# The recurrent block's norm scale applied to projection results instead of to the rows

## The chip, the core and the metric

One core of one Trainium2 chip runs the whole program once. The time is the device time of that core in microseconds (us), the median of several executions; one execution is profiled. The engines are TensorE (PE, with its weight loads as PEld), VectorE (DVE), ScalarE (ACT), GpSimd (POOL) and SyncE (SP, which only issues DMAs here). Each runs its own instructions in order, and they meet at semaphores. Matmul results land in eight PSUM banks.

## What is computed

Two blocks follow each other on x, 256 tokens by 1024 features, float32. Block 1 has two attention layers, each of which ends in `x = x + gate * rms_norm(y, g_post[l])`. Block 2 begins with a recurrent mixer, its feed-forward part, then a second layer with eight experts and a final norm. The place of the change is the seam between layer 1 of block 1 and the recurrent mixer:

```python
def rms_norm_2(x, g):
    y = x * rsqrt(mean(x * x, axis=-1) + EPS)
    return y * g

h = x                                             # what block 1 returned
hn = rms_norm_2(h, norm_mix[0])
proj = hn @ ev_w_in                               # 1024 -> 2568
xr, yr, q, k, v, f_logit = jnp.split(proj, EVEN_SPLITS, axis=-1)   # five of 512, one of 8
xc = causal_depthwise_conv(xr, conv_w, conv_b)    # 4 taps along the tokens
h_lru = rglru(xc, ...)                            # two gates per channel, then a scan over tokens
y_a = h_lru * gelu(yr)
log_f = log_sigmoid(f_logit + f_b)
y_b = fox_attention(q, k, v, log_f)               # 8 heads, cumsum(log_f) added to the scores
h = h + concatenate([y_a, y_b]) @ w_out
```

The norm's factor 1/sqrt(mean + EPS) is one number for each token, so it can be put on the rows before the product or on its result.

## The kernel before

Activations lie transposed, features on partitions: `x`, `h` and their like are eight tiles (k = 0 to 7) of 128 features by 256 tokens. Products are made from two parts of each operand: ACT copies a tile to the reduced type fp32r (the upper part, `hi`), DVE subtracts to get the rest (`lo`), and PE adds three products (`product`, L801 to L805: hi by hi, lo by hi, hi by lo). Weights stream from memory through `ring`, six slots of 1 MB filled by SP. A slot of 256 output columns gives two pieces of 128 columns. `piece_upper(n)` is ACT's part of piece n (L1766) and `piece_lower(n)` DVE's (L2840). Four pairs of part tiles are used in turn (PIECES = 4): ACT may form piece n only when PE is done with piece n-4, and PE starts a projection when its `lo` part is there.

The order on each engine is written out by hand, one section per engine. The PSUM banks are claimed in turn from two groups of four, "gemm" and "attn" (`claim`, L721): PE waits until the last user of the bank has been read by the engine named with the claim.

At the seam the order is this. PE ends layer 1's eight output tiles ("out"), forms the mean of squares of the result ("post") and spreads its inverse root over the partitions (`spread`, L774). DVE multiplies `yo` by it and adds it to `x`, in four pairs of tiles (L2834, L2838). Then comes the norm of the mixer: DVE forms h = x * weight (`weighted`, L2857) for all tiles, ACT the squares (L1763), PE their mean per token (`token_squares`, L763), ACT the root, DVE the reciprocal, PE spreads it. Then h is scaled in place in four pairs (`normed`, L2867), ACT forms their upper parts (`pair_uppers`, L1802) and DVE their lower ones (L2871). In between PE runs idle products on constants (`keep_busy`, L788). After that PE projects: flog (8 outputs spread over 128 rows, plain float32, L748), then xr, yr, qf in four chunks each, the two gates of the recurrence ("lru", 8 small products), kf in four chunks, and vf in two. Each chunk of xr, yr, qf, kf is 24 matmuls into one bank.

Results leave PSUM on ACT (`copy_out`, L1821, and `rows_out`, L2065 and L2066, which puts two heads of 64 rows apart), each followed on ACT by the `piece_upper` that PE's next chunks need. Before the first copy ACT issues nine DMAs for later (`fetch`, L1721: mask, picks, gate weights). DVE meanwhile convolves xr (`convolve`, L2899 and L2901), works on flog and its running sum (L2915 to L2917), and forms the lower parts between these. POOL forms gelu's argument from yr (L3440 to L3444).

## Time and profile before

| | us |
|---|---|
| median of 3 runs | 1960.36 |
| lowest, highest | 1958.73, 1962.9 |
| the profiled execution | 1962.08 |
| its span, first to last instruction | 1958.8 |
| mean granted TensorE clock | 0.988 |

The profile is of one execution. "Busy" is the time in which an engine executes; the time before an instruction in which its engine stood idle is given with what released it. All times below count from the first instruction. The seam lies at 638 to 656 us, the mixer's projections at 656 to 723 us.

### The profile page before, as it was taken

Reading aid. Unit: us, or ns where it says so; the run is one execution under the profiler, and the core shown is the slowest. Engines: PE = TensorE matmul, PEld = TensorE weight load, DVE = VectorE, ACT = ScalarE, POOL = GpSimd, SP = SyncE. Lnnn points to the kernel's source line nnn. Section 1 sums busy time; section 2 is a strip of 40 time slices with the busy share of each in tenths; the row PEclk is TensorE's granted clock in tenths of the full one; section 3 lists DMA queues with packets and bytes.
Section 4 is the critical chain, followed back from the end, with each engine's and each line's share of the span. In section 5 each row is a group of like instructions: output and inputs, shape, how many; then the busy total and the mean of one; then the engine's idle time right before and its main releaser. Section 6 shows DMA issues by size and latency. Waiting matters only on the chain.

```text
span 1958.8 us, 30650 instructions
## 1 busy us (share of the span) xinstructions
PE 1918.3 (98%) x12361; PEld 1570.0 (80%) x12361; DVE 1185.5 (61%) x1698; ACT 969.5 (49%) x1429; POOL 29.8 (2%) x29
## 2 busy tenths in 40 slices
PE   6999999999999999999999999999999999999998
PEld 4999899999899989999999736883588887368833
DVE  4767886565785776666663217951498884059611
ACT  3647753466863575443463206740476673057501
POOL 1000000000000120000000000000000000000000
PEclk7999999999999999999999999999999999999999
DMA  9985556465544542555455899999999999999997
GB/s 291 270 267 184 163 174 160 98 188 189 158 140 140 177 142 88 194 194 158 158 187 203 336 395 407 416 365 412 409 413 409 404 374 347 414 408 411 409 410 303
DMA packets 292565, 536.83 MB, mean 274 GB/s; under 512 B 67076, under 2 KB 198600, under 8 KB 278096
## 3 DMA queue, kind: packets, MB, share of 16 engines
q1 hardware_dynamic: 287968, 530.82, 75.4%
q10 hardware_dynamic: 3920, 3.69, 0.6%
q8 instruction: 98, 1.61, 0.3%
q0 software_dynamic: 544, 0.43, 0.1%
q14 instruction: 35, 0.29, 0.0%
HBM read 533.83 MB, written 1.07 MB: 273 GB/s over the span
## 4 chain that ended last, share of the span: by engine, by line
PE 62%; DMA 2%; DVE 1%; ACT 1%; issue 0%; SPq 0%; DVEq 0%
PE bank L803 14%; PE bank L805 14%; PE bank L804 13%; PE bank L1603 9%; PE bank L1630 4%; DMA pool<-in_od_exp_w 2%; PE bank L1411 1%; PE bank L1458 1%; PE bank L1487 1%; PE bank L1519 1%; PE bank L763 1%; PE bank L748 1%; PE bank L1616 0%; PE bank L788 0%; PE bank L779 0%
## 5 line engine op out<-in xcount | busy, mean ns | idle before, releaser
L3123 DVE TENSOR_TENSOR expert_lo<-pool,w_hi 128x2048 fp32r<-128x2048 f32 x168 | 376.9, 2287 | 46.6 <-ACT w_hi L2268 46.5
L2268 ACT ACTIVATE w_hi<-pool 128x2048 fp32r<-128x2048 f32 x168 | 313.2, 1912 | 29.4 <-DMA pool<-in_od_exp_w 25.3
L803 PE MATMUL bank<-h_upper,upper 128*128 128x256 f32 x1056 | 310.0, 294 | 2.1 <-DVE ring_lo L2537 2.0
L804 PE MATMUL bank<-h_lo,upper 128*128 128x256 f32 x1056 | 300.5, 285 | 0.0
L805 PE MATMUL bank<-h_upper,ring_lo 128*128 128x256 f32 x1056 | 300.4, 284 | 0.0
L2537 DVE TENSOR_TENSOR ring_lo<-ring,upper 128x1024 fp32r<-128x1024 f32 x148 | 179.7, 1222 | 102.9 <-ACT upper L1785 102.6
L803 PEld LDWEIGHTS bank<-h_upper,upper 128*128 128x128 f32 x1056 | 204.1, 193 | 9.6 <-issue 8.5
L804 PEld LDWEIGHTS bank<-h_lo,upper 128*128 128x128 f32 x1056 | 204.3, 193 | 1.0 <-issue 0.4
L805 PEld LDWEIGHTS bank<-h_upper,ring_lo 128*128 128x128 f32 x1056 | 204.1, 193 | 0.0
L1603 PE MATMUL bank<-pool,xe_light 128*64 128x512 f32 (+1 forms) x976 | 187.4, 539 | 2.8 <-issue 2.0
L2847 DVE TENSOR_TENSOR piece_lo<-ring,piece_hi 128x1024 fp32r<-128x1024 f32 x118 | 144.7, 1237 | 73.9 <-ACT piece_hi L1774 73.6
L803 PE MATMUL bank<-w_hi,xe_hi 128*128 128x512 f32 x448 | 178.0, 397 | 2.9 <-DVE expert_lo L3123 2.9
L1785 ACT ACTIVATE upper<-ring 128x1024 fp32r<-128x1024 f32 x148 | 155.1, 1054 | 41.8 <-DMA ring<-in_w_in 24.7
L805 PE MATMUL bank<-w_hi,xe_lo 128*128 128x512 f32 x448 | 174.9, 390 | 0.0
L804 PE MATMUL bank<-expert_lo,xe_hi 128*128 128x512 f32 x448 | 174.3, 389 | 0.0
L1603 PEld LDWEIGHTS bank<-pool,xe_light 128*64 128x64 f32 x976 | 69.1, 137 | 108.4 <-issue 99.3
L1774 ACT ACTIVATE piece_hi<-ring 128x1024 fp32r<-128x1024 f32 x118 | 123.1, 1053 | 51.4 <-PE bank L805 51.2
L803 PEld LDWEIGHTS bank<-w_hi,xe_hi 128*128 128x128 f32 x448 | 84.3, 188 | 24.3 <-DVE expert_lo L3123 4.6
L1630 PE MATMUL bank<-pool,hT_light 128*64 128x512 f32 x448 | 99.9, 594 | 0.0
L803 PE MATMUL bank<-row_hi,piece_hi 128*128 128x256 f32 x352 | 99.9, 284 | 0.0
L804 PE MATMUL bank<-row_lo,piece_hi 128*128 128x256 f32 x352 | 99.6, 283 | 0.0
L805 PE MATMUL bank<-row_hi,piece_lo 128*128 128x256 f32 x352 | 99.6, 283 | 0.0
(482 smaller groups left out, 3605.0 us busy)
## 6 DMA issues: line engine op xcount, KB each, us to landing
pool<-in_od_exp_w SPq DMA_DIRECT2D x330, 1024.0 KB, 13.9
ring<-in_w_in SPq DMA_DIRECT2D x48, 1024.0 KB, 5.7
ring<-in_ev_ffn_w SPq DMA_DIRECT2D x33, 1024.0 KB, 5.3
ring<-in_w_ada SPq DMA_DIRECT2D x24, 1024.0 KB, 7.7
ring<-in_od_w_in SPq DMA_DIRECT2D x12, 1024.0 KB, 5.4
ring<-in_ev_w_in SPq DMA_DIRECT2D x10, 1024.0 KB, 5.4
ring<-in_w_in SPq DMA_DIRECT2D x32, 256.0 KB, 4.5
ring<-in_w_out SPq DMA_DIRECT2D x8, 1024.0 KB, 4.9
```

Source lines behind the costliest of these rows:

```text
L748: m = nc.tensor.matmul(b[base:base + rows, 0:cols], left(k), right(k), start=(k == 0), stop=(k == K - 1))
L803: nc.tensor.matmul(b, left[0], right[0], start=first, stop=False, skip_group_check=True)
L804: nc.tensor.matmul(b, left[0], right[1], start=False, stop=False, skip_group_check=True)
L805: return nc.tensor.matmul(b, left[1], right[0], start=False, stop=last, skip_group_check=True)
L1603: m = nc.tensor.matmul(b[ROOM * j:ROOM * j + ROOM, 0:cols_], xe_light[:, c], t[:, k, cols_ * j:cols_ * j + cols_], start=c == 0, stop=c == ...
L1630: m = nc.tensor.matmul(bank[Y[0]][ROOM * n:ROOM * n + ROOM], t[:, e, ROOM * j:ROOM * j + ROOM], w[:, k, 512 * n:512 * n + 512], start=blk ...
L1774: nc.scalar.activation(piece_tiles(n, *src.shape[1:])[0], src, ACT.Copy)\
L1785: nc.scalar.activation(upper_tile(n), upper_source(n)[0], ACT.Copy)\
L2268: nc.scalar.activation(w_hi[q % HIS], ring_slot(q), ACT.Copy)\
L2537: V.tensor_tensor(dst, src, upper_tile(n).bitcast(F32), ALU.subtract)\
L2847: V.tensor_tensor(lo, src, hi.bitcast(F32), ALU.subtract).then_inc(piece_ready, tick(piece_ready, n))
L3123: V.tensor_tensor(low_slot(q), ring_slot(q), w_hi[q % HIS].bitcast(F32), ALU.subtract)\
```

## The change

The rows of the mixer are no longer scaled. h = x * weight goes into the products as it is, and every result is multiplied by the token's factor when it leaves PSUM. This moves work:

- DVE takes the exits of flog, xr, yr, qf and kf from ACT (`rows_out`, `head_rows_out`, a multiplication of the bank by `rstd[:, 0]`). ACT keeps those of vf, with the factor as its scale, in two halves per tile. ACT's copy of the factor to SBUF is new (`row_root`).
- The four xr chunks are run together, input tile by input tile, each in its own bank, as soon as the parts of a pair of tiles are there (`project_weighted`). The mean of squares is formed between them. flog and the spreading of the factor come after.
- DVE forms h and the lower parts behind each pair of sums of x (`after_sum`). ACT does square and upper part pair by pair.
- The parts of the first four pieces are formed by ACT while the output tiles 3 to 6 of layer 1 run, and by DVE ahead of and behind the reciprocal of "post".
- Piece 4 is formed before, pieces 5 to 7 behind ACT's nine DMAs.
- `yo` gets a place of its own, over the finished gates za and zb, and three banks are claimed from "attn" in place of "gemm".

```diff
@@ -225,7 +225,8 @@
-    z = {b: place(4, S) for b in "abc"}
+    yo = place(8, S)
+    z = {"a": yo[:, 0:4], "b": yo[:, 4:8], "c": place(4, S)}
...
-    yo = qkc
...
-        def spread(key, first, n, freed_by, *step):
+        def spread(key, first, n, freed_by, *step, group="gemm"):
-            b = claim("gemm", ("r", *key, first), freed_by, *step)
+            b = claim(group, ("r", *key, first), freed_by, *step)
...
-        token_squares(("mix", 0))
-        keep_busy(4)
-        spread(("mix", 0), 0, NT, h_ready, "mix", 0, KD - 1)
-        keep_busy(5)
+        def project_weighted(key, *targets):
+            banks = [claim("gemm", (name, c), scaled_rows, name, c) for name, c, _ in targets]
+            for k in range(KD):
+                pe.wait_ge(left_ready, when(left_ready, *key, k))
+                for b, (name, c, tile) in zip(banks, targets):
+                    w = take_piece((tile,), c % 2, KD, P)
+                    m = product(b[:, 0:S], [t[:, k] for t in w], (left_hi[:, k], left_lo[:, k]), k == 0, k == KD - 1)
+                    if k == KD - 1:
+                        m.then_inc(psum_ready, wrote(name, c))
+                        release_piece((tile,), c % 2)
+                mean_square_part(key, k, "attn")
+
+        project_weighted(("mix", 0), *(("xr", c, "xr" + "1" * (c // 2)) for c in range(4)))
         pe.wait_ge(flog_spread, when(flog_spread, "all"))
-        chunk(("flog",), "gemm", clog_ready, ("flog",), KD, lambda k: flogw[:, k], lambda k: h[:, k],
-              fresh=("mix", 0))
+        b = claim("attn", ("flog",), clog_ready, "flog_rows")
+        for k in range(KD):
+            if k == KD // 2:
+                spread(("mix", 0), 0, NT, rstd_row, "mix", 0, group="attn")
+            m = nc.tensor.matmul(b[:, 0:S], flogw[:, k], h[:, k], start=(k == 0), stop=(k == KD - 1))
+        m.then_inc(psum_ready, wrote("flog"))
 
             for c in range(4):
-                project_piece((name + "1" * (c // 2),), c % 2, (name, c), proj_ready,
-                              fresh=("mix", 0) if (name, c) == ("xr", 0) else None)
-
-        project_rows("xr")
+                project_piece((name + "1" * (c // 2),), c % 2, (name, c), scaled_rows)
+
         project_rows("yr")
         project_rows("qf")
...
@@ -2035,17 +2047,20 @@
                     .then_inc(yo_ready, tick(yo_ready, "out", l, c))
                 if c < KD - 1:
                     form_behind(("out", l, c // 2), c % 2)
+                if l == L - 1 and 2 < c < KD - 1:
+                    piece_upper(c - 3)
             token_root("post", l)
-
-        pair_squares(("mix", 0), x, lambda k: (x_ready, when(x_ready, "l", L - 1, k)))
-        for n in range(2):
-            piece_upper(n)
+        for c in range(0, KD, 2):
+            act.wait_ge(x_ready, when(x_ready, "l", L - 1, c + 1))
+            nc.scalar.activation(sq[:, c:c + 2], x[:, c:c + 2], ACT.Square).then_inc(sq_ready, two(sq_ready, "mix", 0, c))
+            act.wait_ge(weighted_step, when(weighted_step, "l", L - 1, c + 1))
+            nc.scalar.activation(left_hi[:, c:c + 2], h[:, c:c + 2], ACT.Copy)\
+                .then_inc(left_hi_ready, two(left_hi_ready, "mix", 0, c))
         token_root("mix", 0)
-        pair_uppers(("mix", 0))
-        for n in range(2, PIECES):
-            piece_upper(n)
+        piece_upper(PIECES)
+        row_root("mix", 0, slot=0)
 
         act.wait_ge(psum_ready, when(psum_ready, "ms", "mix", 0))
         fetch(loaded_block2, mask, C["causal"][:, 0:P])
...
-        def rows_out(name, c, dst):
-            b = psum(act, name, c)
-            nc.scalar.activation(dst[0:HEAD, 0, c], b[0:HEAD, 0:S], ACT.Copy)
-            nc.scalar.activation(dst[HEAD:P, 1, c], b[HEAD:P, 0:S], ACT.Copy)\
-                .then_inc(proj_ready, tick(proj_ready, name, c))
...
-        for c in range(4):
-            copy_out(("xr", c), conv[:, c, 3:3 + S])
+        for c in range(1, 4):
             piece_upper(c + PIECES)
         act.wait_ge(clog_ready, when(clog_ready, "abs"))
         nc.scalar.activation(tmp[:, 0], tmp[:, 0], ACT.Exp, scale=-1.0).then_inc(lru_act, tick(lru_act, "fexp"))
         for c in range(4):
-            copy_out(("yr", c), yr[:, c])
             piece_upper(4 + c + PIECES)
         act.wait_ge(clog_ready, when(clog_ready, "one"))
         nc.scalar.activation(tmp[:, 0], tmp[:, 0], ACT.Ln).then_inc(lru_act, tick(lru_act, "fln"))
         for c in range(4):
-            rows_out("qf", c, qf)
             piece_upper(8 + c + PIECES)
...
-        rows_out("kf", 0, kf)
         piece_upper(12 + PIECES)
         act.wait_ge(lru_dve, when(lru_dve, "loga"))
         nc.scalar.activation(ag, rg, ACT.Exp).then_inc(lru_act, tick(lru_act, "a"))
-        rows_out("kf", 1, kf)
...
-            nc.scalar.activation(vf[:, :, 256 * j:256 * j + 256], b.rearrange("p (t n) -> p t n", t=NT), ACT.Copy)\
-                .then_inc(proj_ready, tick(proj_ready, "vf", j))
+            for t in range(NT):
+                m = nc.scalar.activation(vf[:, t, 256 * j:256 * j + 256], b[:, 256 * t:256 * t + 256], ACT.Copy,
+                                         scale=rtok[:, t:t + 1])
+            m.then_inc(proj_ready, tick(proj_ready, "vf", j))
...
+        def after_sum(c):
+            if c >= 0:
+                for k in (c, c + 1):
+                    weighted(vec("norm_mix_2", k), k, "l", L - 1)
+            if c > 0:
+                pair_lower(("mix", 0), c - 2)
+            if c == KD - 2:
+                pair_lower(("mix", 0), c)
+
+        def pair_lower(key, c):
+            pair = slice(c, c + 2)
+            dve.wait_ge(left_hi_ready, when(left_hi_ready, *key, c + 1))
+            V.tensor_tensor(left_lo[:, pair], h[:, pair], left_hi[:, pair].bitcast(F32), ALU.subtract)\
+                .then_inc(left_ready, two(left_ready, *key, c))
@@ -2826,7 +2865,13 @@
             if l == 0:
                 lower(*both("cq", l + 1), (("ckv", l + 1), 0))
                 shift_gain(1)
+            if l == L - 1:
+                for n in range(PIECES - 1):
+                    piece_lower(n)
             inverse_tokens("post", l)
+            if l == L - 1:
+                dve.wait_ge(psum_ready, when(psum_ready, "out", l, KD - 1))
+                piece_lower(PIECES - 1)
             r = spread_root("post", l)[:, 0:S]
             dve.wait_ge(yo_ready, when(yo_ready, "out", l, KD - 1))
...
-                .then_inc(weighted_step, tick(weighted_step, *ready, c))
+                if l == L - 1:
+                    after_sum(c - 2)
...
-        for c in range(KD):
-            weighted(vec("norm_mix_2", c), c, "l", L - 1)
-        piece_lower(0)
-        normed(("mix", 0), parts=True, behind=lambda: piece_lower(1))
-        for n in range(2, PIECES):
-            piece_lower(n)
+        inverse_tokens("mix", 0)
+        piece_lower(PIECES)
         link(V.memset(conv[:, :, 0:3], 0.0))
-
+        dve.wait_ge(rstd_row, when(rstd_row, "mix", 0))
+
+        def rows_out(name, c, *dsts):
+            b = psum(dve, name, c)
+            for rows, dst in dsts:
+                m = V.tensor_tensor(dst, b[rows, 0:S], rstd[rows, 0], ALU.mult)
+            m.then_inc(scaled_rows, tick(scaled_rows, name, c))
+
+        def head_rows_out(name, c, dst):
+            rows_out(name, c, *((slice(HEAD * e, HEAD * e + HEAD), dst[HEAD * e:HEAD * e + HEAD, e, c]) for e in range(2)))
+
+        every = slice(0, P)
+        for c in range(4):
+            rows_out("xr", c, (every, conv[:, c, 3:3 + S]))
+        piece_lower(1 + PIECES)
         b = psum(dve, "flog")
-        V.tensor_scalar(clog, b[:, 0:S], fb, None, ALU.add).then_inc(clog_ready, tick(clog_ready, "flog"))
+        V.tensor_tensor(clog, b[:, 0:S], rstd[:, 0], ALU.mult).then_inc(clog_ready, tick(clog_ready, "flog_rows"))
+        dve.wait_ge(clog_ready, when(clog_ready, "flog_rows"))
+        V.tensor_scalar(clog, clog, fb, None, ALU.add).then_inc(clog_ready, tick(clog_ready, "flog"))
         dve.wait_ge(clog_ready, when(clog_ready, "flog"))
...
         for c in range(4):
-            piece_lower(c + PIECES)
+            if c > 1:
+                piece_lower(c + PIECES)
             convolve(c)
         dve.wait_ge(lru_act, when(lru_act, "fexp"))
         V.tensor_scalar(tmp[:, 0], tmp[:, 0], 1.0, None, ALU.add).then_inc(clog_ready, tick(clog_ready, "one"))
         for n in range(4, 8):
+            rows_out("yr", n - 4, (every, yr[:, n - 4]))
             piece_lower(n + PIECES)
         dve.wait_ge(lru_act, when(lru_act, "fln"))
...
         for n in range(8, 12):
+            head_rows_out("qf", n - 8, qf)
             piece_lower(n + PIECES)
...
+        head_rows_out("kf", 0, kf)
         piece_lower(12 + PIECES)
...
         for n in range(13, 16):
+            head_rows_out("kf", n - 12, kf)
             piece_lower(n + PIECES)
...
-        pool_engine.wait_ge(proj_ready, when(proj_ready, "yr", 3))
+        pool_engine.wait_ge(scaled_rows, when(scaled_rows, "yr", 3))
         pool_engine.wait_ge(lru_dve, when(lru_dve, "conv", 3))
```

The functions `piece_lower`, `left_lower` and `weighted` are moved up in DVE's section, unchanged. Waits on `proj_ready` for the results that DVE now reads become waits on the new semaphore `scaled_rows`.

PE, from the spreading of "post" in layer 1 to xr. `ident,mean1024` are idle products, `mean1024,sq` the means of squares, `ident,small` spreads a factor, `h,pool` is flog. Before:

```order
L779 MATMUL bank0<-ident,small 128x128 x2
L788 MATMUL bank4<-ident,mean1024 128x128 x12
L763 MATMUL bank1<-mean1024,sq 128x1 x16
L788 MATMUL bank4<-ident,mean1024 128x128 x4
L779 MATMUL bank2<-ident,small 128x128 x2
L788 MATMUL bank4<-ident,mean1024 128x128 x5
L748 MATMUL bank3<-h,pool 128x256 x8
L803 MATMUL bank0<-left_hi,piece_hi 128x256
```

After, from the end of the last xr chunk to the first yr product:

```order
L806 MATMUL bank0<-left_hi,piece_lo 128x256
L764 MATMUL bank4<-mean1024,sq 128x1 x2
L1181 MATMUL bank5<-h,pool 128x256 x4
L780 MATMUL bank6<-ident,small 128x128 x2
L1181 MATMUL bank5<-h,pool 128x256 x4
L804 MATMUL bank1<-left_hi,piece_hi 128x256
```

The xr products stood behind flog and now stand ahead of it; their banks are 1, 2, 3 and 0, and bank 0 is the one in which the factor of "post" was spread. (A float32 product of the order is two in the trace.)

ACT, from the last root of layer 1 to the first exits. `small<-bank` is a root, `sq<-x` the squares, `left_hi` and `piece_hi` the upper parts of rows and of weights. Before:

```order
L1763 ACTIVATE sq<-x 128x512 x4
L1774 ACTIVATE piece_hi<-ring 128x1024 x2
L1812 ACTIVATE small<-bank1,small 128x2
L1802 ACTIVATE left_hi<-h 128x512 x4
L1774 ACTIVATE piece_hi<-ring 128x1024 x2
L1721 DMA pool<-const_causal 128x128
L1721 DMA pool<-const_pick 32x1024 x4
L1721 DMA pool<-in_ev_ga_w_2 64x4x64 x2
L1721 DMA pool<-in_ev_gx_w_2 64x4x64 x2
L1821 ACTIVATE pool<-bank0 128x256
L1774 ACTIVATE piece_hi<-ring 128x1024
```

The same place after (line numbers of the changed file):

```order
L2059 ACTIVATE left_hi<-h 128x512
L1824 ACTIVATE small<-bank4,small 128x2
L1786 ACTIVATE piece_hi<-ring 128x1024
L1809 ACTIVATE rstd<-bank6 128x256
L1733 DMA pool<-const_causal 128x128
L1733 DMA pool<-const_pick 32x1024 x4
L1733 DMA pool<-in_ev_ga_w_2 64x4x64 x2
L1733 DMA pool<-in_ev_gx_w_2 64x4x64 x2
L1786 ACTIVATE piece_hi<-ring 128x1024 x3
```

The nine DMAs now stand behind an instruction that needs the spread factor, and the parts of pieces 5 to 7 behind them.

DVE, from the last lower part of the rows to the second convolution. Before:

```order
L2847 TENSOR_TENSOR piece_lo<-ring,piece_hi 128x1024 x2
L2889 MEMSET pool 128x4x3
L2892 TENSOR_SCALAR pool<-bank,small 128x256
L2894 SCALAR_TENSOR_TENSOR tmp<-pool 128x256
L2847 TENSOR_TENSOR piece_lo<-ring,piece_hi 128x1024
L2899 TENSOR_SCALAR pool<-pool,vecs 128x256
L2901 SCALAR_TENSOR_TENSOR pool<-pool,vecs 128x256 x3
L2847 TENSOR_TENSOR piece_lo<-ring,piece_hi 128x1024
```

After:

```order
L2912 MEMSET pool 128x4x3
L2918 TENSOR_TENSOR pool<-bank,rstd 128x256 x4
L2540 TENSOR_TENSOR piece_lo<-ring,piece_hi 128x1024
L2929 TENSOR_TENSOR pool<-bank,rstd 128x256
L2931 TENSOR_SCALAR pool<-pool,small 128x256
L2933 SCALAR_TENSOR_TENSOR tmp<-pool 128x256
L2938 TENSOR_SCALAR pool<-pool,vecs 128x256
L2940 SCALAR_TENSOR_TENSOR pool<-pool,vecs 128x256 x3
L2938 TENSOR_SCALAR pool<-pool,vecs 128x256
L2940 SCALAR_TENSOR_TENSOR pool<-pool,vecs 128x256 x3
L2540 TENSOR_TENSOR piece_lo<-ring,piece_hi 128x1024
```

Ahead of the first convolution there are now four exits of xr and the lower part of piece 5; the lower parts of pieces 6 and 7 stand behind the second and the third convolution.

## Rows read from the trace of the kernel before

**Rows 1.** The page, busy time, share of the span and instructions, by engine.

```profile
PE 1918.3 (98%) x12361; PEld 1570.0 (80%) x12361; DVE 1185.5 (61%) x1698; ACT 969.5 (49%) x1429; POOL 29.8 (2%) x29
```

**Rows 2.** Stretches: length, busy (instructions) of PE, PEld, DVE, ACT, POOL; PEclk; DMA.

```profile
644.20:656.10 11.90, 11.46 (x71) 10.64 (x71) 11.20 (x23) 6.66 (x11) 0.95 (x1) 0.86 0.43 137
656.10:690.80 34.70, 34.70 (x290) 34.67 (x289) 28.87 (x37) 20.79 (x31) 9.85 (x5) 1.00 0.57 177
690.80:696.40 5.60, 3.60 (x19) 2.85 (x17) 3.38 (x6) 5.31 (x11) 5.52 (x2) 1.00 0.74 241
```

**Rows 3.** Timeline of PE: start, duration, line, count, [idle before <- releaser].

```profile
640.88 0.61 PE L779 MATMUL bank<-ident,small 128*128 128x128 f32 x4
641.33 2.84 PE L788 MATMUL bank<-ident,mean 128*128 128x128 f32 x24
...
652.82 3.62 PE L748 MATMUL bank<-h,pool 128*128 128x256 f32 x16
656.09 0.47 PE L803 MATMUL bank<-left_hi,piece_hi 128*128 128x256 f32 x1
```

**Rows 4.** Timeline of DVE at the seam, same columns.

```profile
641.53 1.28 DVE L2834 TENSOR_TENSOR pool<-pool,bank 128x512 f32<-128x512 f32 x2 [0.98 <-PE bank L779]
...
644.54 0.68 DVE L2834 TENSOR_TENSOR pool<-pool,bank 128x512 f32<-128x512 f32 x1
645.13 1.29 DVE L2838 TENSOR_TENSOR x<-x,pool 128x512 f32<-128x512 f32 x2
646.34 2.19 DVE L2857 TENSOR_SCALAR h<-x,vecs 128x256 f32<-128x256 f32 x8
```

**Rows 5.** Timeline of PE in layer 1's output tiles: a mean of squares among products.

```profile
624.80 0.28 PE L805 MATMUL bank<-h_upper,ring_lo 128*128 128x256 f32 x1
624.92 0.50 PE L763 MATMUL bank<-mean,sq 128*128 128x1 f32 x4
625.29 0.36 PE L803 MATMUL bank<-h_upper,upper 128*128 128x256 f32 x1
```

**Rows 6.** Timeline of PE, then stretches: a wait and the granted clock behind it.

```profile
123.01 0.36 PE L803 MATMUL bank<-h_upper,upper 128*128 128x256 f32 x1 [2.01 <-DVE ring_lo L2537]
...
124.14 0.42 PE L804 MATMUL bank<-h_lo,upper 128*128 128x256 f32 x1
124.35 0.41 PE L805 MATMUL bank<-h_upper,ring_lo 128*128 128x256 f32 x1
...
124.00:127.00 3.00, 3.00 (x16) 3.00 (x16) 2.96 (x5) 2.15 (x3) 0.00 (x0) 0.50 1.10 349
```

**Rows 7.** Timeline of ACT and its DMA issues (ACTq) before the first exit.

```profile
655.28 0.37 ACTq L1721 DMA_DIRECT2D pool<-const_causal  x1
...
659.70 1.41 ACTq L1721 DMA_DIRECT2D pool<-in_ev_gx_w  x2
661.16 0.38 ACT L1821 ACTIVATE pool<-bank 128x256 f32<-128x256 f32 x1 [3.43 <-issue]
```

**Rows 8.** Timeline of DVE during xr, yr and qf.

```profile
663.66 0.41 DVE L2899 TENSOR_SCALAR pool<-pool,vecs 128x256 f32<-128x256 f32 x1
664.11 1.53 DVE L2901 SCALAR_TENSOR_TENSOR pool<-pool,vecs 128x256 f32<-128x256 f32 x3
665.55 1.22 DVE L2847 TENSOR_TENSOR piece_lo<-ring,piece_hi 128x1024 fp32r<-128x1024 f32 x1
...
682.87 1.26 DVE L2915 SCALAR_TENSOR_TENSOR tmp<-pool,tmp 128x256 f32<-128x256 f32 x1
...
686.68 3.17 DVE L2847 TENSOR_TENSOR piece_lo<-ring,piece_hi 128x1024 fp32r<-128x1024 f32 x2
```

**Rows 9.** Timeline of PE around the gates and before vf.

```profile
694.71 1.99 PE L748 MATMUL bank<-pool 128*128 128x256 f32 x8 [2.00 <-ACT pool L2071]
696.36 0.47 PE L803 MATMUL bank<-left_hi,piece_hi 128*128 128x256 f32 x1
...
709.04 0.35 PE L803 MATMUL bank<-piece_hi,left_hi 128*128 128x256 f32 x1 [0.83 <-DVE piece_lo L2847]
```

38 lines of the change are left out of this document (19 added, 19 removed).

## The prediction

> **What bounds the kernel now.** I read the page's busy shares first: PE is busy 98% of the span, every other engine 61% or less [rows 1]. So time can be won or lost only where PE waits, runs filler, or runs slowly. Then I read the stretches around the seam. From 644.2 to 656.1 us PE is called busy for 11.46 of 11.9 us, yet none of it but the spreading and flog is work that a result needs: the rest is means of one column and idle products, at a granted clock of 0.86. DVE, busy 11.20 of 11.9 us, sets the pace [rows 2]. From 656.1 to 690.8 PE runs xr, yr and qf without a wait, and **DVE is already busy for 28.87 of these 34.7 us**, ACT for 20.79 [rows 2]. That is the number on which the forecast turns, since the change takes work off ACT and puts it on DVE. After that PE waits 2.00 us for ACT's first gate [rows 9]. Behind vf the order does not change much, and what the seam gains or loses is passed on: the weights of the experts are fetched when PE's progress lets them.
>
> **Part 1, the start of xr.** Now the first xr product starts at 656.09 [rows 3]. After the change it needs the parts of tiles 0 and 1 and four free banks, one of them the bank from which DVE reads the factor of "post" until its fourth yo product. DVE's chain now begins at 641.53; a pair product or sum costs 0.60 from start to start (645.13 minus 644.54), eight weightings 2.1, so 0.26 each [rows 4]. The lower part of piece 3 is put ahead of the chain where DVE stands idle for 0.98 us; it takes 1.22, so the chain starts 0.1 later, at 641.64. The fourth yo product, at 644.54 now, gets in front of it two weightings (0.52 and some 0.13 for a semaphore on DVE's own result), twice, and one lower part of a pair (0.60): 644.54 + 0.1 + 0.65 + 1.25 = 646.55, done at 647.25. The parts of tiles 0 and 1 are there at 646.7, so the bank decides, and **PE starts xr at 647.3**. Behind it DVE delivers the other pairs by 649.1, 651.0 and 651.8, each ahead of PE.
>
> **Part 2, the length of xr.** 96 products at 0.12 (624.80 to 624.92 [rows 5]) are 11.5 us. Eight means of squares stand among them: 0.37 each until the next product starts and 0.08 that this one is late, 0.45 [rows 5], together 3.6. Before it PE is idle from 644.2, the end of the filler [rows 3], for 3.1 us. After a wait of 2.01 us at 121 to 123 the granted clock was 0.50 from 124 to 127, that is 1.2 GHz instead of 2.4, and products stood 0.21 apart instead of 0.12 [rows 6]; 3 us hold 14 of them instead of 25, which loses 1.3 us, and with the ends of the slow time I take 1.5. A wait of 2.00 us before the gates brought no fall, the clock stayed at 1.00 [rows 2, 9]. The wait here is half as long again, so I count 1.5 and keep 0 for the range. xr ends at T = 647.3 + 11.5 + 3.6 + 1.5 = **663.9 us**. Before it ended at 656.1 + 11.5 = 667.6, so 3.7 us seem won. But flog (3.3, from 652.82 to 656.09) and the spreading (0.45, 640.88 to 641.33) now come behind [rows 3]; with some 0.2 for the changes between kinds of product yr can start at T + 4.0 = 667.9, the old time. **The rearrangement alone wins nothing if the clock falls, 1.5 us if it doesn't.**
>
> **Part 3, ACT's DMA issues.** Before, the nine issues ran from 655.28 to 661.11, 5.83 us, in which ACT's next instruction could not start (3.43 us idle, "issue"), while PE had pieces 0 to 3 in hand [rows 7]. Now they stand behind `row_root`, which waits for the spread factor: half of flog and the spreading, T + 2.3. They end at T + 8.2. Only then can ACT form the upper part of piece 5, for which I take 1.1 since it is as long as DVE's lower part of 1.22 or somewhat shorter [rows 8], and DVE that lower part: **T + 10.4**. PE has done yr's first chunk, on piece 4, at T + 4.0 + 2.9 = T + 6.9 and waits 3.5 us for the second. DVE too has nothing to do from the exits of xr (T + 2.9 to T + 4.4) until T + 9.3, since piece 5 stands first in its queue; flog, the convolutions and everything up to kf are queued behind it.
>
> The Trainium skill, page "DMA: Bandwidth & Descriptors", section "Issuing engines are not separate DMA queues", says that the time an engine's sequencer spends on initiating DMAs is usually small relative to the DMA itself. The row differs: 0.65 us for each of nine issues. By the page's rule this stall would not exist and the result would be that of rival B below.
>
> **Part 4, DVE's queue.** From T + 10.45, start to start: flog's three instructions, each waiting for the one before, 1.3 (0.45 each: 663.66 to 664.11); two convolutions, 1.89 each (663.66 to 665.55), so T + 15.6; piece 6, 1.13, T + 16.7, and only now can PE start yr's third chunk; convolution, piece 7, convolution, 1.89 + 1.13 + 1.89: T + 21.65; one small instruction 0.2 [rows 8]. (A piece lasts 1.22 but the next instruction starts some 0.1 earlier, as the sums of rows 4 do.) Then four times an exit of yr and a piece. An exit, a product of a bank of 256 columns with SBUF, is not in the trace: half of L2834's 0.60 bounds it below, the 0.45 between dependent instructions above [rows 4, 8]; I take 0.35. 4 x (0.35 + 1.13) = 5.9: T + 27.8. The logarithm's sum and scan, 682.87 to 686.68: 3.8 [rows 8], T + 31.6. Exits of qf are two each (64 rows, as long as 128): three times 0.70 + 1.13, and 0.70, 6.2; and POOL's argument of gelu, which waits for the fourth exit of yr, now falls into this stretch, beside which two pieces took 3.17 instead of 2.35 [rows 8]: 1.0 more. **The fourth bank of qf is free at T + 38.9.** PE ended qf at about T + 35 and needs that bank for the fourth gate product. Then 0.47, and from the first product of the second gate to kf 1.65 (694.71 to 696.36 [rows 9]): kf starts at T + 41.0 = 704.9. ACT's table load and first gate let PE go on 3.9 us after the end of qf now (690.8 to 694.71 [rows 9]), two copies of 0.38 [rows 7] less in the changed kernel: T + 38.1, hidden.
>
> **Sum.** kf starts at 704.9 instead of 696.36 [rows 9]: **+8.5 us**. In kf DVE gets four double exits, 3 us, but it is busy with little there, ACT is freed of four copies, and the lower part on which vf waits (709.04, 0.83 us idle [rows 9]) comes as long after kf as now, within 0.5. vf's exit in two halves costs ACT some 0.3 beside PE's work. I count both at nothing, with 1 us to the range. The profiled execution took 1962.08 (span 1958.8), 1.7 above the median 1960.36; 8.5 on its own time is 1970.6, and on the median **1968.9 us**.
>
> **Rivals.**
> - A, the forecast: DVE's queue and ACT's issues hold PE back; +5 to +11 us by the exit's bounds, the clock and POOL.
> - B: the issues don't hold piece 5 back (they are quicker, or overlap), so DVE starts at T + 4.4 instead of T + 9.3 and only its own load counts: 8.5 - 4.9 = +3.6, that is 1964; with a faster exit or no fall of the clock down to +1.5. Against it speaks ACT's 3.43 us of idle time [rows 7].
> - C, the other side: not slower. DVE has 5.8 us to spare in 34.7 [rows 2], and the waits that I add up would have to be hidden: PE goes from flog through yr and qf without one. Then yr starts at T + 4.0 without the clock's fall, 666.4 against 667.6, and ACT gets to its gates 0.8 earlier, without two 0.38 copies [rows 7]: -2.0 us, 1958.4. It decides at DVE: the change adds there (4 + 4 + 8) x 0.35 + 0.4 = 6.0 us until the end of qf, more than the spare 5.8, and DVE starts later. So I give it little.
> - D: the waits bring more slow clock. PE waits three times for 2 to 3.5 us, and a slow stretch that falls into kf or behind the gates costs 1.5 each: +11 to +15.
>
> **Chances.** A 0.58, B 0.20, C 0.12, D 0.10. A measurement of this kernel can tell about 0.2%, 3.9 us, from no change. Slower by more: A, D and half of B, 0.77. Within it: most of C and the rest of B, 0.20. Faster by more: 0.03, since even C wins only 2 us. The range leaves out C's gain and D's upper end: 1962.4 (+2) to 1973.8 (+13.4).
>
> **What will show it.** In the changed profile: the first xr product near 647.3, the last near 663.9, a granted clock of 0.5 between them; ACT's nine issues from about 666 to 672 with idle time behind them; PE waiting for `piece_lo` before the second and third chunk of yr; DVE without a gap from there to the gates; kf's first product near 705. The prediction is wrong if PE passes from flog to qf's end without a wait, or if POOL or ACT release kf later than DVE does.

## The result

| | before | after |
|---|---|---|
| median | 1960.25 (4 runs, 1958.73 to 1962.9) | 1973.49 (4 runs, 1971.69 to 1976.85) |
| ratio, 95% interval | | 1.0067 (1.0053 to 1.0081) |
| profiled execution | 1962.08 | 1971.69 |
| its span | 1958.8 | 1969.6 |

The change makes the kernel 13.1 us slower. The forecast was 1968.9 with a range of 1962.4 to 1973.8.

PE is still the engine that is busy nearly always; what was lost hardly shows in the page's first lines. First the page, then four stretches of the changed kernel (length, busy and instructions of PE, PEld, DVE, ACT, POOL, then the granted share of full clock, and DMA), which answer to [rows 1, 2]:

```profile
PE 1918.9 (97%) x12343; PEld 1568.0 (80%) x12343; DVE 1191.3 (60%) x1719; ACT 963.3 (49%) x1408; POOL 31.3 (2%) x29
...
646.35:662.90 16.55, 16.55 (x128) 16.55 (x129) 3.96 (x9) 2.52 (x4) 0.00 (x0) 0.90 0.29 92
662.90:705.40 42.50, 34.78 (x230) 32.07 (x230) 34.85 (x56) 20.47 (x26) 16.21 (x7) 0.92 0.49 149
...
648.00:652.00 4.00, 4.00 (x25) 4.00 (x25) 2.35 (x5) 1.26 (x2) 0.00 (x0) 0.64 0.74 233
...
676.00:680.00 4.00, 2.54 (x13) 2.27 (x12) 3.86 (x8) 2.05 (x3) 0.00 (x0) 0.73 0.59 209
...
700.00:704.00 4.00, 2.53 (x8) 1.90 (x7) 3.92 (x5) 2.79 (x6) 3.92 (x2) 0.76 0.70 246
```

During xr (646.35 to 662.90) PE works without a gap, and DVE and ACT have next to nothing to do. In the 42.5 us behind it PE stands idle for 7.7 us, and there are three stretches of reduced clock in all.

PE of the changed kernel (start, duration, line, count, idle time before it and what ended it), which answers to [rows 3, 9]:

```profile
640.13 2.84 PE L789 MATMUL bank<-ident,mean 128*128 128x128 f32 x24
646.35 0.36 PE L804 MATMUL bank<-left_hi,piece_hi 128*128 128x256 f32 x1 [3.37 <-DVE pool L2879]
...
662.54 0.50 PE L764 MATMUL bank<-mean,sq 128*128 128x1 f32 x4
662.90 1.97 PE L1181 MATMUL bank<-h,pool 128*128 128x256 f32 x8
...
673.74 0.38 PE L804 MATMUL bank<-left_hi,piece_hi 128*128 128x256 f32 x1 [3.82 <-DVE piece_lo L2540]
...
679.83 0.38 PE L804 MATMUL bank<-left_hi,piece_hi 128*128 128x256 f32 x1 [1.47 <-DVE piece_lo L2540]
...
701.72 4.08 PE L749 MATMUL bank<-pool 128*128 128x256 f32 x10 [1.47 <-DVE pool L2918]
705.42 0.51 PE L804 MATMUL bank<-left_hi,piece_hi 128*128 128x256 f32 x1
...
718.43 0.36 PE L804 MATMUL bank<-piece_hi,left_hi 128*128 128x256 f32 x1 [1.11 <-DVE piece_lo L2540]
```

The first xr product waits for DVE to read a bank; yr's second and third chunk (673.74, 679.83) wait for lower parts; the fourth gate product waits for DVE's exit of qf. Every wait ends at DVE. Why DVE is late stands in its own timeline and in ACT's, which answer to [rows 7, 8]:

```profile
663.37 0.17 DVE L2514 RECIPROCAL small<-small 128x2 f32<-128x2 f32 x1 [12.77 <-ACT small L1824]
...
665.83 1.42 DVE L2918 TENSOR_TENSOR pool<-bank,rstd 128x256 f32<-128x256 f32 x4 [0.27 <-DVE pool L2912]
672.46 1.23 DVE L2540 TENSOR_TENSOR piece_lo<-ring,piece_hi 128x1024 fp32r<-128x1024 f32 x1 [5.21 <-ACT piece_hi L1786]
...
690.67 0.42 DVE L2956 SCALAR_TENSOR_TENSOR tmp<-pool,tmp 128x256 f32<-128x256 f32 x1
691.21 0.27 DVE L2957 MEMSET rstd<- 128x256 f32 x1
691.51 1.88 DVE L2958 TENSOR_TENSOR_SCAN pool<-rstd,tmp 128x256 f32<-128x256 f32 x1
693.31 0.83 DVE L2918 TENSOR_TENSOR pool<-bank,rstd 64x256 f32<-64x256 f32 x2
...
700.72 0.86 DVE L2918 TENSOR_TENSOR pool<-bank,rstd 64x256 f32<-64x256 f32 x2
```

```profile
665.37 0.36 ACTq L1733 DMA_DIRECT2D pool<-const_causal  x1
...
669.06 2.21 ACTq L1733 DMA_DIRECT2D pool<-in_ev_gx_w  x2
671.37 2.95 ACT L1786 ACTIVATE piece_hi<-ring 128x1024 fp32r<-128x1024 f32 x3 [5.63 <-issue]
```

DVE idles 12.77 us during xr, forms the four exits, then waits 5.21 us for ACT, which is issuing DMAs from 665.37 to 671.27. From 672.46 to 703 it has no gap.

### The profile page after: what moved, and what is told of

Its sections match the earlier page's. It is cut to its first block, busy times and chain, and to the rows that moved or that the text cites. A ratio compares the mean times of both kernels' runs of the same rounds, so it can differ in the third digit from the quotient of the medians.

```text
span 1969.6 us, 30620 instructions
## 1 busy us (share of the span) xinstructions
PE 1918.9 (97%) x12343; PEld 1568.0 (80%) x12343; DVE 1191.3 (60%) x1719; ACT 963.3 (49%) x1408; POOL 31.3 (2%) x29
## 3 DMA queue, kind: packets, MB, share of 16 engines
q10 hardware_dynamic: 3920, 3.69, 0.6%
## 4 chain that ended last, share of the span: by engine, by line
PE 88%; DVE 5%; DMA 4%; ACT 1%; issue 1%; ACTq 1%; SPq 0%; DVEq 0%
PE bank L804 20%; PE bank L806 20%; PE bank L805 20%; PE bank L1615 9%; PE bank L1642 4%; DMA pool<-in_od_exp_w 2%; PE bank L749 2%; PE bank L764 1%; PE bank L1423 1%; PE bank L1470 1%; DVE piece_lo L2540 1%; PE bank L959 1%; PE bank L1499 1%; PE bank L947 1%; PE bank L981 1%; DMA ring<-in_w_in 1%
## 5 line engine op out<-in xcount | busy, mean ns | idle before, releaser
L1615 PEld LDWEIGHTS bank<-pool,xe_light 128*64 128x64 f32 x976 | 69.9, 138 | 109.3 <-issue 100.5
L804 PE MATMUL bank<-left_hi,piece_hi 128*128 128x256 f32 x320 | 94.9, 297 | 9.1 <-DVE piece_lo L2540 5.7
```

What stands on the lines that cost most here:

```text
L804: nc.tensor.matmul(b, left[0], right[0], start=first, stop=False, skip_group_check=True)
L1615: m = nc.tensor.matmul(b[ROOM * j:ROOM * j + ROOM, 0:cols_], xe_light[:, c], t[:, k, cols_ * j:cols_ * j + cols_], start=c == 0, stop=c == ...
```

## One mark for all runs

The experiments move things by a few microseconds, and the start of this seam differs by 6 us from one execution to the next. So places are given from a mark M, PE's last mean of squares of layer 1 (sixteen steps; 638.21 in the kernel before, 637.01 after). T is the end of xr, kf and vf stand for the first product of these projections, "ffn" the table load of ACT behind the mixer's output (746.40 and 756.12). T is left open for the kernel before, whose xr stands in another place. The last column is the measured ratio times 1960.

| kernel | T | kf | vf | ffn | ffn, against before | measured, against before (95%) |
|---|---|---|---|---|---|---|
| before | | 58.2 | 70.8 | 108.2 | | |
| after | 25.9 | 68.4 | 81.4 | 119.1 | +10.9 | +13.1 (10.4 to 15.9) |
| after again | 26.8 | 69.6 | 82.5 | 120.3 | +12.1 | +13.1 (10.8 to 15.7) |
| 1 fetches early | 27.1 | 62.6 | 75.6 | 113.3 | +5.1 | +5.5 (3.1 to 7.8) |
| 2 fillers | 24.4 | 67.0 | 79.9 | 117.6 | +9.4 | +8.0 (5.5 to 10.6) |
| 3 exits on ACT | 25.9 | 67.1 | 80.6 | 117.9 | +9.8 | +11.8 (8.4 to 15.1) |
| 4 = 1 and 3 | 27.0 | 63.0 | 75.7 | 113.0 | +4.8 | +5.1 (2.7 to 7.4) |
| 5 = 1, 2, reordered | 24.4 | 61.8 | 75.5 | 113.2 | +5.0 | +6.3 (3.9 to 8.8) |
| 6 = 1 and 2 | 24.4 | 61.1 | 74.5 | 112.2 | +4.1 | +2.9 (0.8 to 5.1) |
| 7 fetches late | 25.6 | 62.4 | 75.8 | 113.5 | +5.3 | +9.6 (6.1 to 13.1) |
| 8 = 6, conv on ACT | 24.4 | 59.8 | 72.8 | 110.5 | +2.3 | +1.6 (-0.2 to 3.3) |
| 9 = 8, other order | 24.4 | 56.2 | 69.9 | 107.6 | -0.6 | -1.6 (-3.5 to 0.4) |
| 10 = 6, gate fillers | 24.4 | 61.0 | 74.0 | 111.7 | +3.5 | +1.8 (-0.2 to 3.7) |
| 11 = 9, kf's order | 24.4 | 56.2 | 67.9 | 105.6 | -2.6 | -2.0 (-3.7 to -0.2) |

The mark's difference agrees with the measured one within its interval everywhere but in run 7, where it is 0.8 us below. So the loss arises between M and kf and is carried to the end. From "ffn" to the end the profiled executions take 1209.7 to 1221.0 us, one execution for each kernel and without any order in it; that is the noise that the marks avoid. A mark is itself one execution, and the granted clock at one place differs from execution to execution.

## The experiments

Theory: ACT's block of issues and DVE's queue, in this order, hold PE back. Rivals: the load of DVE alone; the clock; only PE's own longer xr.

### Runs 1 and 7: where the nine fetches stand

```diff
+        act.wait_ge(psum_ready, when(psum_ready, "ms", "post", L - 1))
+        fetch(loaded_block2, mask, C["causal"][:, 0:P])
...
         token_root("mix", 0)
         piece_upper(PIECES)
         row_root("mix", 0, slot=0)
-        act.wait_ge(psum_ready, when(psum_ready, "ms", "mix", 0))
-        fetch(loaded_block2, mask, C["causal"][:, 0:P])
...
```

All nine fetches go there; POOL's clearing of the gate weights' place waits for the same earlier mark.

> The changed kernel with one edit: ACT's nine weight fetches of the mix stage stand ahead of its root of the token's mean square, instead of behind the root of the row's, and wait for layer 1's last mean of squares instead of the mix stage's. Nothing is left out. Theory 1 (the block of nine issues, 667 to 671 in the changed kernel's frame, holds the pieces of yr's rows, and through them the queue of DVE): DVE's first lower piece behind the block no longer waits 5.21 us for ACT, the convolutions and exits behind it come about 5 us earlier, kf's first product about 5 us earlier, and the time is about 5 us below the changed kernel's (0.9975 of it, +8 us against the kernel before instead of +13). Theory 2 (DVE's added work alone, exits, pieces and log sum in one queue, sets the end, and fills the time that the issues leave): DVE is busy where it waited, kf's first product moves by less than 1 us, ratio to the changed kernel 1.000. Theory 3 (the fetches collide with others when they start earlier): a wait for a weight tile appears and the time rises.

Measured: 1965.07, ratio 1.0028 (1.0016 to 1.0040), which is 7.6 us below the changed kernel where some 5 were expected, and vf and kf are 5.8 us earlier from M. ACT, DVE and PE of this run:

```profile
652.56 1.31 ACTq L1733 DMA_DIRECT2D pool<-in_ev_gx_w  x2
663.88 0.26 ACT L1824 ACTIVATE small<-bank,small 128x2 f32<-128x2 f32 x1 [14.43 <-PE bank L764]
...
666.44 2.94 ACT L1786 ACTIVATE piece_hi<-ring 128x1024 fp32r<-128x1024 f32 x3
```

```profile
667.96 1.22 DVE L2540 TENSOR_TENSOR piece_lo<-ring,piece_hi 128x1024 fp32r<-128x1024 f32 x1
669.09 0.42 DVE L2929 TENSOR_TENSOR pool<-bank,rstd 128x256 f32<-128x256 f32 x1
```

```profile
675.33 0.39 PE L804 MATMUL bank<-left_hi,piece_hi 128*128 128x256 f32 x1 [1.74 <-DVE piece_lo L2540]
...
697.23 2.40 PE L749 MATMUL bank<-pool 128*128 128x256 f32 x10 [1.47 <-DVE pool L2918]
699.27 0.47 PE L804 MATMUL bank<-left_hi,piece_hi 128*128 128x256 f32 x1
```

The issues now end at 653.87 and fall where ACT has nothing else (14.43 us idle before the root). DVE's wait of 5.21 us is gone, and PE's waits of 3.82 and 1.47 have become one of 1.74. The lone wait for a piece that is left belongs to DVE's order: two convolutions stand ahead of piece 6.

The 5.8 us are not the block alone. From T, kf is 6.95 us earlier (T+35.57 against T+42.52). Of this 1.66 is the clock at the gates: from the first of the ten gate records to kf it is 2.04 us here at a granted clock of 1.00 (697.23 to 699.27) and 3.70 in the changed kernel (701.72 to 705.42). That leaves **5.3 us for the block**, and a longer slow stretch in xr took 1.2 back before T.

Run 7 leaves xr alone and puts the fetches behind later pieces instead, two or three at a time:

```diff
         for c in range(4):
             piece_upper(4 + c + PIECES)
+            for to, source in later[2 * c:2 * c + 3 if c == 3 else 2 * c + 2]:
+                fetch(loaded_block2, to, source)
```

> The changed kernel with the nine fetches late instead of early: two behind each of the upper pieces 4, 5 and 6 and three behind piece 7, where ACT has 1.5 to 3.5 us idle, so that none stands ahead of pieces 1 to 3. All is computed. If it is the block of issues ahead of yr's pieces that costs, and not where the fetches go: vf's first product comes 5 to 6 us earlier than in the changed kernel, as with early fetches, and the clock of xr is as in the changed kernel (that much less to lose: 6 to 7 us). If the early fetches won by something else (the gate weights landing earlier, POOL's clearing earlier): no gain here, or a new wait for the gate weights ahead of the gates' products.

vf comes 5.6 us earlier from M, as in run 1, with PE's waits much the same (1.73 and 0.43, then 0.54 and 1.47 at the gates). From T, kf is 5.73 us earlier, and the gate records with their slow clock take 3.26 to kf instead of 3.70, which leaves 5.3 for the block here too. So it is the block ahead of the pieces that costs, and not the place of the fetches. Of the time itself this run says less: ratio 1.0049 (1.0031 to 1.0067), 4 us more than its mark. Whether late fetches cost something behind "ffn" stays open.

### Run 2, and the kernel again: the clock ahead of xr

```diff
             spread(("post", l), 0, NT, dve_step, "yo", l, KD - 2)
-            keep_busy(12)
+            keep_busy(24 if l == L - 1 else 12)
```

> The changed kernel with one edit: twenty-four filler products of TensorE in place of twelve behind layer 1's spreading of the mean of squares, so that TensorE is busy through its wait of 3.37 us ahead of xr. Nothing is left out. If the slow clock of 648 to 652 (granted 0.64) costs time on the path to kf: that stretch shows 0.9 or more, xr ends about 1.5 us earlier, and kf's first product and the end move by 1.5 us (1972 instead of 1973.5). If xr's end is set by something else, or if the fillers only displace products or move the slow stretch to a later place: no change, at most 0.3 us.

> The changed kernel itself, unedited, on the same chip as the three that stand beside it, so that their distance to it is read without a chip between. Expected: 1.0067 of the kernel before (between 1.005 and 1.008), that is 13 us.

Stretches of both, first with the longer filler, then the changed kernel in another execution:

```profile
648.00:652.00 4.00, 4.00 (x37) 4.00 (x36) 1.82 (x4) 1.24 (x2) 0.00 (x0) 1.00 0.63 197
```

```profile
648.00:652.00 4.00, 3.47 (x17) 3.50 (x17) 3.80 (x9) 2.52 (x4) 0.00 (x0) 0.50 1.10 348
```

With PE busy up to 0.69 us before xr, the clock stays at 1.00 and xr takes 15.0 us instead of 16.55: **1.5 us**, and vf moves by 1.5. The ratio is 1.0041 (1.0028 to 1.0054), 5 us below the changed kernel where the mark gives 1.5. The changed kernel in another execution ran at 0.50 for longer (xr 17.5 us, 2.5 more than with the filler) and had kf 1.1 us later from M. So how much slow clock an execution meets differs. The six profiles without the longer filler have an xr of 16.3 to 17.7 us, 17.0 in the mean, and the seven with it 15.0 each, so the filler saves some 2.0 in the mean. The rest of the 5 us no profile here explains.

### Runs 3 and 4: the exits on ACT

```diff
-            rows_out("yr", n - 4, (every, yr[:, n - 4]))
+            plain_out("yr", c, (slice(0, P), yr[:, c]))
```

The first line is DVE's, a multiplication by the factor, the second ACT's, a copy. The same for qf and kf. So runs 3 and 4 leave out the factor of these three, and their results are not the program's.

> The changed kernel with the exits of yr, qf and kf from PSUM moved from DVE to ACT, as plain copies. It leaves out the multiplication of yr's, qf's and kf's results by the norm's factor. Theory 1 (DVE's queue is the bound from xr's end to kf's first product): DVE loses 4 x 0.35 + 4 x 0.89 + kf's exits, ACT gains as much where it has slack; kf's first product comes 2 to 4 us earlier, and the time is 2 to 4 us below the changed kernel's. Theory 2 (the fetches' issues on ACT are the bound): ACT, with still more in its queue behind the issues, makes nothing earlier: the time is as the changed kernel's or up to 2 us above.

> Both edits together: ACT's nine weight fetches ahead of its root of the token's mean square, and the exits of yr, qf and kf on ACT as plain copies, so that the norm's factor is left out of these three. If the issues on ACT and the exits on DVE together are what the change costs, kf's first product comes about 9.7 us earlier than in the changed kernel, and the time is within 2 us of the kernel before's. If the two only hide each other (either alone sets the end), each alone gives little and both give the 9 to 10. If the slow clock ahead of xr, the later start of the recurrence's gates or a contention of POOL and DVE on the way has a share of its own, 3 us or more stay above the kernel before.

Run 3 gives 0.8 us at vf, against 2 to 4 expected (ratio 1.0060, 1.0043 to 1.0077), and run 4 gives no more than run 1 alone (1.0026, 1.0014 to 1.0038). The reason is in PE's timeline of run 4:

```profile
695.09 1.99 PE L749 MATMUL bank<-pool 128*128 128x256 f32 x8 [2.00 <-ACT pool L2089]
```

That line's releaser is ACT's gate: what PE waits for is again the gate on ACT, 2.00 us, as in [rows 9]. ACT now has qf's last exit, a piece (692.19 to 693.25) and a table load (1.28) ahead of its first gate at 694.56. Taking 5 us of work from one queue and putting it in the other only moved the last wait. Ahead of the gates nothing was to be won either: both runs wait 1.73 or 1.74 us for piece 6, and their first gate product stands at T+30.5. My expectation for run 4 (9.7 us at kf) added up what DVE would be rid of and left ACT's queue out.

### Runs 5 and 6: both cheap cures, and a first reordering

Run 6 has the edits of runs 1 and 2 and nothing else.

> The changed kernel with the nine fetches early and twenty-four fillers ahead of xr. All is computed. With the early fetches alone vf's first product came 5.8 us earlier from the mark, though xr ended 1.2 us later by a longer slow stretch. If the slow clock ahead of xr adds to the issues' cost: vf 8.5 us earlier than in the changed kernel, the time 2 to 3 us below that with early fetches alone, and 2 to 4 us above the kernel before. If the gain of a faster xr is taken up by DVE's queue: vf moves by less than 1 us against early fetches alone.

Measured: 1962.13, ratio 1.0015 (1.0004 to 1.0026), vf 6.9 us earlier than in the changed kernel, "ffn" +4.1 against before. The two add up, though not fully at vf (5.8 and 2.7 were expected, 1.6 more): a slow stretch at the gates and the start of kf took that back, which run 1 had been spared. It costs 1.15 up to kf (3.19 us instead of 2.04 from the first of the ten records) and 0.5 between kf and vf (13.46 instead of 12.97).

Run 5 adds another order on DVE and ACT: pieces between the convolutions, the log gate's three steps behind yr's third exit.

> The changed kernel with the nine fetches early, twenty-four fillers ahead of xr, and another order on DVE and ACT: lower pieces go between the convolutions (two convolutions ahead of yr's exits, two between them), the log gate's steps behind yr's third exit, its scan behind qf's pieces. All is computed. If issues, slow clock and the order of DVE's queue are the whole of the loss: vf's first product stands about 10 us earlier than in the changed kernel from the same mark (the projections' last mean of squares of layer 1's output stage), and the time is within 2 us of the kernel before's. If DVE's load is what counts and not its order: it stands where the run with early fetches and fillers alone has it. If PE's longer xr (3.6 us of means of squares between its products) can't be hidden by anything: at least 3 us above the kernel before stay.

vf came 5.9 us earlier than in the changed kernel instead of the 10 expected, and kf is 0.7 us later than in run 6; ratio 1.0032 (1.0020 to 1.0045). ACT and DVE of run 5:

```profile
683.10 0.42 ACT L2086 ACTIVATE tmp<-tmp 128x256 f32<-128x256 f32 x1 [5.68 <-DVE tmp L2944]
683.42 1.99 ACT L1786 ACTIVATE piece_hi<-ring 128x1024 fp32r<-128x1024 f32 x2
```

```profile
684.50 1.97 DVE L2540 TENSOR_TENSOR piece_lo<-ring,piece_hi 128x1024 fp32r<-128x1024 f32 x1 [1.10 <-ACT piece_hi L1786]
```

I had put DVE's steps late that feed ACT's Exp, and the upper pieces are queued behind that Exp: ACT stood still for 5.68 us, and DVE then waited for ACT. The mistake is that of the change itself, made once more: a short instruction that waits, with the pieces behind it.

### Runs 8 to 11: the load and the order of DVE's queue

Run 8 is run 6 with the first step of the four convolutions on ACT; run 10 is run 6 with fillers at the gates.

```diff
-            link(V.tensor_scalar(xc[:, c], conv[:, c, 0:S], vec("ev_conv_w_2", c), vec("ev_conv_b_2", c), ALU.mult, ALU.add))
...
+            nc.scalar.activation(xc[:, c], conv[:, c, 0:S], ACT.Identity, scale=vec("ev_conv_w_2", c),
+                                 bias=vec("ev_conv_b_2", c)).then_inc(lru_act, tick(lru_act, "first", c))
```

> The kernel with early fetches and twenty-four fillers, and the first step of each of the four convolutions on ACT instead of DVE (four steps of 0.44 us, start to start, less in DVE's queue; ACT has idle stretches there). All is computed. If DVE's queue between xr's end (T) and qf's last exit sets kf's start: kf's first product comes 1.8 us earlier, at T+34.9 instead of T+36.7, and the time is 1.0006 of the kernel before instead of 1.0015. If the queue has slack and waits for PE or ACT itself (as where the exits were moved to ACT, which brought 0.8 us at vf): less than 0.5 us.

Measured: kf at T+35.4 instead of T+36.7, ratio 1.0008 (0.9999 to 1.0017). PE of run 8:

```profile
690.07 4.04 PE L749 MATMUL bank<-pool 128*128 128x256 f32 x10 [1.48 <-DVE pool L2922]
693.76 0.47 PE L804 MATMUL bank<-left_hi,piece_hi 128*128 128x256 f32 x1
```

From the first of the ten records to kf it is 3.69 us, 0.5 more than in run 6: more of the slow stretch falls ahead of kf. With that the 1.3 us at kf are the 1.8 expected, and at vf, behind the slow stretch in both, the difference is 1.8. So DVE's load counts from xr's end on, once ACT's block is out of the way.

```diff
+                if g == 0 and c > 1:
+                    keep_busy(8)
                 chunk(("lru", g, c), "gemm", lru_act, ("gate", g, c), 1, lambda k: lru_w[:, g, c], lambda k: xc[:, c])
```

> The kernel with early fetches and twenty-four fillers, and eight filler products of TensorE ahead of each of the third and fourth gate product, where PE waits 0.5 and 1.5 us for DVE's exit of qf. All is computed. If the slow clock behind that wait (granted 0.62 in that stretch) costs: the stretch shows 0.9 or more, kf's first product comes 1 to 1.4 us earlier against qf's fourth exit, and the time goes from 1.0015 to 1.0008 of the kernel before. If the wait of 1.5 us isn't what brings the clock down, or the gates' exits on ACT (0.4 each) pace the products anyway: kf moves by less than 0.4 us.

PE of run 6, then of run 10:

```profile
690.72 3.75 PE L749 MATMUL bank<-pool 128*128 128x256 f32 x10 [1.47 <-DVE pool L2918]
693.91 0.78 PE L804 MATMUL bank<-left_hi,piece_hi 128*128 128x256 f32 x1
```

```profile
693.52 1.95 PE L789 MATMUL bank<-ident,mean 128*128 128x128 f32 x16
695.31 2.32 PE L749 MATMUL bank<-pool 128*128 128x256 f32 x10
697.28 0.47 PE L804 MATMUL bank<-left_hi,piece_hi 128*128 128x256 f32 x1
```

From the first of the ten records to kf it is 1.97 us at full clock instead of 3.19, so the slow clock costs 1.2 us up to kf and 0.5 more in it. But the fillers run past DVE's exit (693.16 to 694.02) and hold the gates up by 1.15, from T+33.53 to T+34.68: kf moved by 0.1 from M instead of the 1 to 1.4 expected, vf by 0.6. Ratio 1.0009 (0.9999 to 1.0019).

Run 9 puts DVE's queue in another order, on top of run 8: pieces 5 to 7 ahead of the convolutions, the last two convolutions behind yr's first two exits and their pieces, qf's third and fourth exit back to back, the scan last.

> The same with DVE's queue in another order: yr's lower pieces 1 to 3 ahead of the convolutions, convolutions 2 and 3 behind yr's first two exits, qf's third and fourth exit back to back, and the log gate's scan behind all of them. All is computed. By DVE's queue: qf's fourth exit starts at about T+28.3 instead of T+32.5, PE waits for none of yr's or qf's pieces, the gates end at about T+33, kf's first product at T+33.2; with the marks behind it that gives 3.5 us below the kernel with early fetches and fillers, 0.9997 of the kernel before (0.9985 to 1.001). If POOL's work falls on the same pieces and scan and makes them slower, as in the first reordered kernel: T+36, no gain. If the recurrence behind kf is later for the later scan: kf gains and vf or the scores behind it give it back.

PE, then DVE of run 9:

```profile
691.80 1.99 PE L749 MATMUL bank<-pool 128*128 128x256 f32 x8 [1.26 <-ACT pool L2080]
693.44 0.47 PE L804 MATMUL bank<-left_hi,piece_hi 128*128 128x256 f32 x1
...
707.13 0.35 PE L804 MATMUL bank<-piece_hi,left_hi 128*128 128x256 f32 x1 [1.83 <-DVE piece_lo L2544]
```

```profile
688.84 0.86 DVE L2922 TENSOR_TENSOR pool<-bank,rstd 64x256 f32<-64x256 f32 x2 [0.59 <-PE bank L806]
...
692.86 0.69 DVE L2972 TENSOR_TENSOR_SCAN pool<-rstd,tmp 128x256 f32<-128x256 f32 x1
```

DVE now waits for PE at qf's fourth chunk, and PE for no piece of yr or qf and only 1.26 us at the gates. kf starts at T+31.8 instead of T+35.4 with the same instructions. **The order alone is worth 3.6 us at kf**, in two parts: behind the wait of 1.26 the clock held at 1.00, which gives back the 1.65 us that it cost in run 8 (3.69 instead of 2.04), and 2.0 is the shorter way through the queue. Ratio 0.9992 (0.9982 to 1.0002). What is late next is vf, by DVE's piece behind kf's second exit. Run 11 moves that one pair:

```diff
+        head_rows_out("kf", 1, kf)
+        piece_lower(13 + PIECES)
         dve.wait_ge(lru_act, when(lru_act, "tanh"))
```

> The kernel with early fetches, fillers, ACT's first convolution steps and DVE's other order (0.9992 of the kernel before), with one more step moved: DVE's exit of kf's second chunk and the lower piece behind it stand ahead of the two steps of the recurrence that wait 2.60 us for ACT's tanh, instead of behind them. All is computed. If DVE's queue is still what makes PE wait 1.83 us ahead of vf's first product: that wait goes, vf's first product and all behind it come 1.8 us earlier (vf 68.0 us from the mark instead of 69.9), and the time is 0.9983 of the kernel before (0.9973 to 0.9993). If the recurrence's own steps are next: vf comes earlier, the output projection behind it does not, and the time stays at 0.9992.

```profile
698.14 0.86 DVE L2922 TENSOR_TENSOR pool<-bank,rstd 64x256 f32<-64x256 f32 x2 [0.50 <-PE bank L806]
```

```profile
703.70 0.28 PE L804 MATMUL bank<-piece_hi,left_hi 128*128 128x256 f32 x1
```

The wait ahead of vf is gone, vf and "ffn" come 2.0 us earlier. The ratio is 0.9990 (0.9981 to 0.9999): **with the fetches early, fillers ahead of xr, four convolution steps on ACT and DVE's queue in another order, the change is about 2 us faster than the kernel before** (0.2 to 3.7 by the interval, only just clear of nothing), instead of 13 us slower. Against run 9 alone the times don't tell it apart; the marks do.

From the changed kernel to run 9 kf moved by 12.2 us from M, and the runs, with one profile each, split it: ACT's block 5.3 (runs 1 and 7), the clock in xr 1.5 (run 2), the clock at the gates 1.7 (run 1), DVE's load 1.8 (run 8), DVE's order 2.0 (run 9). No rival was the whole of it. PE's own longer xr is no floor: it is still 15.0 us in run 9, and kf stands 2.0 us earlier from M than in the kernel before.

## Why the prediction was right, and what it missed

The measured median, 1973.49, lies only 0.3 us below the upper end of the range. The mechanism was foreseen step by step, the size less well.

- **Start of xr.** Forecast 647.3; 646.35 plus the 1.20 us by which M is earlier is 647.55. The bank that DVE reads for its last yo product decided, as said.
- **Length of xr.** Forecast 16.6 (11.5 + 3.6 + 1.5), measured 16.55. Run 2 splits it: 15.0 without the slow clock. That the slow clock cost just 1.5 was in part luck: another execution of the same kernel lost 2.5.
- **ACT's issues.** Forecast T+2.3 to T+8.2 and piece 5 at T+10.4; measured T+2.5 to T+8.4 and T+10.8. PE waited 3.82 instead of 3.5. Rival B (1964 without them) is what run 1 made real: 1965.07. The block cost 5.3 us at kf with the clocks set equal. The Trainium skill, page "DMA: Bandwidth & Descriptors", section "Issuing engines are not separate DMA queues", calls the time for initiating a DMA usually small relative to the DMA itself. The trace agrees as far as that goes: 0.65 us for an issue, 1.8 to 3.0 us until these DMAs landed. Part 3 weighed it as if no stall followed from it, and rightly went by the row instead: for nine issues on end ahead of another engine's work the measurement decides against such a reading.
- **DVE's queue.** The scan stage began at T+27.8, exactly as summed, and qf's fourth bank was free at T+38.7 (forecast 38.9). That the end fits so well is luck, since inside terms were off and cancel: the log sum took 2.64 instead of 3.8. A double exit with what follows took 0.89 instead of 0.70; the prediction had its 64 rows as long as 128, rightly, but counted each half at 0.35 from start to start, where it was 0.43 and more. The pieces between took 1.26 instead of 1.13. The 1.0 for POOL's work was right, one piece of 2.23.
- **From there to kf.** This term was mis-sized. Forecast 2.1 us after the fourth exit, measured 3.8: the gates ran at reduced clock, 3.70 us from the first of the ten records to kf against 2.04 in run 1. The prediction put such a stretch into rival D with a chance of 0.10 and gave no reason for so little; [rows 9], where a wait of 2.00 us brought no fall, is its only row on the place. Runs 5 and 6 lost the clock there too, behind waits of 1.5 us, and run 1 didn't. One row in which the clock held was no reason to leave it out.
- **Behind kf.** Counted at nothing; it was 0.3 to vf (the wait of 0.83 became 1.11) and 0.3 more to "ffn", inside the 1 us that the range allowed.

The forecast was 8.5, the marks say 10.9, the measurement 13.1. Of the first gap 1.7 is the gates' clock, less 0.2 by which qf's bank was free early; 0.6 lies behind kf, 0.2 in T. Of the second, the profiled execution was the fastest of the four, and the other profile of the same kernel has a longer slow stretch in xr and a mark of +12.1. What is left, 1 us, is inside the interval. The mechanism of rival A held at every step, but its bounds (+5 to +11) hold the marks' 10.9 only just and not the measured 13.1. That lies in rival D's bounds (+11 to +15), and D's mechanism was at work too: of its two slow stretches the one at the gates cost 1.7, and the one in yr (676 to 680) nothing, since PE was waiting for DVE there anyway. So what happened is A with a part of D, to which 0.10 was too little.

Rival C (not slower) is what runs 9 and 11 made of the same change with other orders of the queues, fillers and four steps on ACT. So most of the loss lies in where the fetches, fillers and DVE's steps stand, and 1.8 us in DVE's load, which ACT could take; both were undone with the factor still on the results. Whether the kernel before would gain from run 11's order too was not tried.

## What to carry to other kernels

When work moves from one engine's queue to another's, write down both queues in order and look for short instructions that wait (an issue of a DMA, one activation on a result not yet there) ahead of work that another engine needs; run 5 shows how easily one is put back. Moving DMA issues into an idle stretch was worth 5.3 us here, and the order of one queue 3.6, of which 1.65 is slow clock that went with the waits. Load counts as well, if it goes where there is room: 1.8 us moved in run 8 gave 1.8, while 5 us moved in run 3 gave 0.8, because the other queue was next. And before a difference between two runs is given to an edit, compare the granted clock in the stretches between the marks: in run 1 it made up 1.66 us, and in run 8 it hid 0.5.
